# Block kernel, delta-rule layers: z and output units reordered behind the rule, and three taps per chunk moved out of it

## The reference, cut to what matters

```
h = rms_norm(x, norm_w);  proj = h @ w_in
qkv, z_a, a_lg, b_lg, cf_val, cf_glu, z_b, gate_lg = split(proj)
# delta-rule branch: a 5 tap convolution, 4 heads of 128, both directions
o = gated_delta_chunked(forward) + flip(gated_delta_chunked(backward))
o = o * rsqrt(mean(o * o, per head) + EPS) * dn_norm_w
y_a = (o * silu(z_a)) @ w_dn_out
# convolution branch: 31 taps along the sequence, per channel
u = cf_val * sigmoid(cf_glu)
u = depthwise_conv_centred(u, cf_conv_w) + cf_conv_b
u = silu(layer_norm(u, cf_ln_w, cf_ln_b))
y_b = (u * silu(z_b)) @ w_cf_out
y = gate_0 * y_a + gate_1 * y_b        # gates: sigmoid of gate_lg + bias
x = x + y @ w_out
```

## Time and profile before

| | us |
|---|---|
| median of 3 runs | 2148.33 |
| profiled execution | 2147.76 |
| its span (first to last instruction) | 2146.4 |
| PE busy in the span | 2067.1 (96%) |
| DVE / ACT / POOL busy | 1246.9 / 858.8 / 906.3 |
| layer 0: rule, then z and output units | about 1366 to 1512, 1512 to 1619 |
| layer 1: the same, 473.03 later | about 1839 to 1985, 1985 to 2092 |

### The profile page before, as it was taken

One profiled execution on the slowest core, in us unless ns is written; L12 is line 12 of the kernel. 1 busy time (PEld: TensorE's weight loads), 2 busy tenths in 40 slices (PEclk: granted clock), 3 DMA queues, 4 the chain that ended last, 5 costly groups with the idle time before them and its releaser, 6 DMA issues.

```text
span 2146.4 us, 26716 instructions
## 1 busy us (share of the span) xinstructions
PE 2067.1 (96%) x10774; PEld 1645.1 (77%) x10774; DVE 1246.9 (58%) x1943; ACT 858.8 (40%) x1373; POOL 906.3 (42%) x431
## 2 busy tenths in 40 slices
PE   9999999998999999999999899999999999999997
PEld 7888888775666688888888677787778787778775
DVE  6322223847677633222224988989753779898753
ACT  4222223324444543222234475444444375344632
POOL 4444444332213344444443564544434554444442
PEclk9999999999999999999999999999999999999999
DMA  4343333321101232333332222101223222100222
GB/s 160 109 136 98 98 98 101 106 69 40 31 25 56 69 98 89 98 98 98 98 96 91 78 79 69 59 31 31 69 80 97 89 81 77 50 25 26 79 89 78
DMA packets 46186, 169.09 MB, mean 79 GB/s; under 512 B 5232, under 2 KB 6000, under 8 KB 45808
## 3 DMA queue, kind: packets, MB, share of 16 engines
q1 hardware_dynamic: 45344, 165.60, 24.8%
q10 hardware_dynamic: 720, 1.79, 0.2%
HBM read 165.27 MB, written 2.10 MB: 78 GB/s over the span
## 4 chain that ended last, share of the span: by engine, by line
PE 74%; DVE 18%; ACT 5%; issue 1%; POOL 0%; DMA 0%; ACTq 0%; DVEq 0%
PE ps L385 21%; PE ps L386 21%; PE ps L387 21%; DVE cu L1843 4%; DVE blk_t L1945 2%; DVE outer L1943 1%; PE ps L639 1%; PE ps L655 1%; PE ps L624 1%; PE ps L441 1%; ACT whi L1009 1%; ACT dl L1441 1%; PE ps L959 1%; DVE dl L2052 1%; PE ps L970 1%
## 5 line engine op out<-in xcount | busy, mean ns | idle before, releaser
L2172 POOL TENSOR_TENSOR wlo<-raw,whi 128x1024 fp32r<-128x1024 f32 x300 | 750.9, 2510 | 863.9 <-ACT whi L1009 863.3
L385 PE MATMUL ps<-xh,whi 128*128 128x512 f32 x1584 | 640.3, 404 | 11.4 <-ACT gates L1185 6.2
L387 PE MATMUL ps<-xh,wlo 128*128 128x512 f32 x1584 | 619.7, 391 | 0.0
L386 PE MATMUL ps<-xl,whi 128*128 128x512 f32 x1584 | 619.3, 391 | 0.0
L1009 ACT CAST whi<-raw 128x1024 fp32r<-128x1024 f32 x300 | 312.6, 1044 | 167.9 <-DMA raw<-in_stream 167.8
L385 PEld LDWEIGHTS ps<-xh,whi 128*128 128x128 f32 x1584 | 298.6, 189 | 105.1 <-issue 32.3
L387 PEld LDWEIGHTS ps<-xh,wlo 128*128 128x128 f32 x1584 | 298.4, 188 | 63.6
L386 PEld LDWEIGHTS ps<-xl,whi 128*128 128x128 f32 x1584 | 298.9, 189 | 59.4 <-issue 2.9
L1843 DVE SCALAR_TENSOR_TENSOR cu<-up,lcols,cu 128x512 f32<-128x512 f32 x180 | 173.3, 1015 | 0.1
L2208 POOL TENSOR_TENSOR cu<-cu,prod 128x512 f32<-128x512 f32 x60 | 87.7, 1461 | 139.6 <-ACT prod L1252 138.5
L1548 DVE TENSOR_TENSOR ml<-mid,mh 128x512 fp32r<-128x512 f32 x42 | 57.5, 1372 | 151.5 <-ACT mh L1071 151.5
(11 more groups left out here) (360 smaller groups left out, 3000.8 us busy)
## 6 DMA issues: line engine op xcount, KB each, us to landing
raw<-in_stream SPq DMA_DIRECT2D x300, 512.0 KB, 3.6
w1k<-in_w SPq DMA_DIRECT2D x1, 2048.0 KB, 8.2
w1v<-in_w SPq DMA_DIRECT2D x1, 2048.0 KB, 8.1
outT<-h SPq DMA_DIRECT2D x4, 512.0 KB, 2.7
h<-in_xT SPq DMA_DIRECT2D x2, 512.0 KB, 7.9
h<-in_xT ACTq DMA_DIRECT2D x2, 512.0 KB, 7.5
mats<-in_mats ACTq DMA_DIRECT2D x1, 448.0 KB, 10.5
msk<-in_masks SPq DMA_DIRECT2D x1, 258.0 KB, 3.8
```

The lines of the kernel that those rows point to most:

```text
L385: pe.matmul(out, wh, hi, start=first, stop=False)
L386: pe.matmul(out, wh, lo, start=False, stop=False)
L387: return pe.matmul(out, wl, hi, start=False, stop=last)
L2172: pool.tensor_tensor(m.wlo[:, slot, :], m.raw[:, slot, :], m.whi[:, slot, :].bitcast(F32), ALU.subtract).then_inc(s.wlo)
```

## The change

1. `POINT_TAPS`: 11 taps a chunk instead of 14. The one at "decay" goes, "join1" 2 to 1, "keys" 4 to 3. `delta` returns the rest of the list.
2. The 8 output units of a layer become 4 of w_dn_out (41 to 44, called D0 to D3) and 4 of w_cf_out (48 to 51, C0 to C3). Each holds 2 column tiles by 4 tiles of the sum, again 24 matmuls. The order of units is now z0 to z4, D0 to D3, z5 to z7, C0 to C3, M0 to M7.
3. DVE behind the rule: 26 taps (2 of the last chunk, 24 more), `o_dn`, `times_z` with 2 taps before the last, `low_part` of `o`, and then 14 taps between the multiplications of the first gates with D0 to D3. In `merge` only the second product is left for each c.
4. PE's sums for the mean stand behind D3 instead of between z3 and z4, and only z5 is left between them and those for the variance.
5. ACT: `split_rows` of `o` directly after z3; casts of weights between c pairs in `merge`, one for each C unit. The mixer's merge of the first block keeps its form.

```diff
-L_QKV, L_GATE, L_Z, L_OUT, L_MERGE = 8, 20, 36, 44, 52
+L_QKV, L_GATE, L_Z, L_DN, L_CF, L_MERGE = 8, 20, 36, 41, 48, 52
...
-POINT_TAPS = {"decay": 1, "level1": 1, "join1": 2, "level2": 1, "join2": 2, "last": 1, "keys": 4, "out": 2}
+POINT_TAPS = {"level1": 1, "join1": 1, "level2": 1, "join2": 2, "last": 1, "keys": 3, "out": 2}
...
+
+
+def z_unit_at(l, n):
+    return U0_LAYER[l] + L_Z + n + (4 if n > 4 else 0)
...
# TensorE
+    def branch_unit(l, i, r):
+
+        u = U0_LAYER[l] + (L_DN, L_CF)[r] + i
+        pe.wait_ge(s.wlo, u + 1)
+        if i >= 2 and r == 0:
+            pe.wait_ge(s.sg, 16 + 8 * l + 2 * i - 2)
+        elif i >= 2:
+            pe.wait_ge(s.ysum, 8 + 8 * l + 2 * i - 2)
+        for rows in (range(3), (3,)):
+            for half in range(2):
+                for k in rows:
+                    if i == 0 and half == 0:
+                        pe.wait_ge(s.mix_lo, 8 + 8 * l + 4 * r + k + 1)
+                    ins = multiply(u, 4 * half + k, ps[:, 2 * (i % 2) + half, :], m.fh[:, 4 * r + k, :], m.fl[:, 4 * r + k, :],
+                                   k == 0, k == 3)
+        ins.then_inc(s.unit)
+
...
@@ -832,16 +860,18 @@
         z_unit(2)
         spread(3 * l + 3, range(4))
         z_unit(3)
+        z_unit(4)
+        pe.wait_ge(s.o_dn, 4 * l + 4)
+        for i in range(4):
+            branch_unit(l, i, 0)
         pe.wait_ge(s.conv, 3 * l + 3)
         pe.wait_ge(s.shared, 30 * l + 30)
         sum_rows(ps[:, 5, :], [m.cu[:, c, :] for c in range(4)]).then_inc(s.mean)
-        z_unit(4)
         z_unit(5)
         pe.wait_ge(s.cu_sq, 4 * l + 4)
         sum_rows(ps[:, 5, :], [m.rt[:, c, :] for c in range(4)]).then_inc(s.var)
         z_unit(6)
         z_unit(7)
-        pe.wait_ge(s.o_dn, 4 * l + 4)
 
     def gate_tiles(l, n, t0, t1):
 
...
# ScalarE
@@ -1374,14 +1404,16 @@
         z_unit(2)
         z_unit(3)
         weights_upto(u0 + L_Z + 4 + AHEAD + 1)
+        for k in range(4):
+            split_rows(k)
+        z_unit(4)
+        for i in range(4):
+            weights_upto(u0 + L_DN + i + AHEAD + 1)
         for c in range(4):
             act.wait_ge(s.cu_c, 4 * l + c + 1)
             act.activation(m.rt[:, c, :], m.cu[:, c, :], ACT.Square).then_inc(s.cu_sq)
-        z_unit(4)
         z_unit(5)
-        for k in range(4):
-            split_rows(k)
-        weights_upto(u0 + L_Z + 6 + AHEAD + 1)
+        weights_upto(z_unit_at(l, 6) + AHEAD + 1)
         act.wait_ge(s.var, l + 1)
         then(act.activation(ps[:, 5, :], ps[:, 5, :], ACT.Ln, bias=eps, scale=1.0 / (4 * P)))
         act.activation(ps[:, 5, :], ps[:, 5, :], ACT.Exp, scale=-0.5).then_inc(s.root_cu)
...
-            weights_upto(u0 + c + AHEAD + 1)
+            weights_upto(u0 + (c if mixer else c // 2) + AHEAD + 1)
...
# VectorE, merge
             p, bank = c % 2, 2 * (c % 2)
             if mixer:
                 dve.wait_ge(s.sg, 2 * c + 2)
+                dve.wait_ge(s.unit, u0 + c + 1)
             else:
-                dve.wait_ge(s.filled, 24 * g - 24 + (2 * c + 2))
-            dve.wait_ge(s.unit, u0 + c + 1)
+                dve.wait_ge(s.unit, u0 + c // 2 + 1)
             sg = [m.m1_sg[:, p, r, :] if mixer else m.sg[:, 2 * c + r, :] for r in range(2)]
-            for r in range(2):
-                t = step(dve.tensor_tensor(sg[r], sg[r], ps[:, bank + r, :], ALU.mult))
+            for r in range(2) if mixer else (1,):
+                at = bank + r if mixer else c % 4
+                t = step(dve.tensor_tensor(sg[r], sg[r], ps[:, at, :], ALU.mult))
...
-        delta(l, cf_tap)
+        taps = delta(l, cf_tap)
+
+        def conv(n):
+            for ch, k in taps[0:n]:
+                cf_tap(ch, k)
+            del taps[0:n]
+
+        conv(24)
...
@@ -2020,15 +2060,25 @@
             dve.wait_ge(s.z_used, 8 * l + n + 1)
             dve.tensor_tensor(m.fl[:, n, :], src, m.fh[:, n, :].bitcast(F32), ALU.subtract).then_inc(s.mix_lo)
 
+        for n in range(4):
+            if n == 3:
+                conv(2)
+            times_z(n)
+        for n in range(4):
+            low_part(n)
+        for c in range(KD):
+            if c % 2 == 0:
+                conv(4)
+                dve.wait_ge(s.filled, 24 * l + 2 * c + 4)
+                dve.wait_ge(s.unit, u0 + L_DN + c // 2 + 1)
+            dve.tensor_tensor(m.sg[:, 2 * c, :], m.sg[:, 2 * c, :], ps[:, c % 4, :], ALU.mult).then_inc(s.sg)
+        conv(len(taps))
+        dve.wait_ge(s.sg, 16 + 8 * l + 8)
         dve.wait_ge(s.conv, 3 * l + 3)
         dve.wait_ge(s.mean, l + 1)
         for c in range(4):
             dve.scalar_tensor_tensor(out=m.cu[:, c, :], in0=ps[:, 5, :], scalar=-1.0 / (4 * P), in1=m.cu[:, c, :],
                                      op0=ALU.mult, op1=ALU.add).then_inc(s.cu_c)
-        for n in range(4):
-            times_z(n)
-        for n in range(4):
-            low_part(n)
         dve.wait_ge(s.root_cu, l + 1)
         for c in range(4):
             dve.tensor_tensor(m.cu[:, c, :], m.cu[:, c, :], ps[:, 5, :], ALU.mult).then_inc(s.cu_n)
```

More of the change, by code:

```diff
@@ L709, in attention, with mixer_branches @@
         gates(turns + 1)
[L711 to L715, removed]
+    def branch_unit(l, i, r):
[13 more added lines that the diff above has]
+        ins.then_inc(s.unit)
+    def mixer_branches():
+        u0 = U0_MIX + 32
         for c in range(KD):
@@ L718, in merge @@
             if c >= 2:
-                pe.wait_ge(s.ysum, 8 * g + c - 1)
+                pe.wait_ge(s.ysum, c - 1)
             pe.wait_ge(s.wlo, u0 + c + 1)
@@ L723, in merge @@
                     if c == 0:
-                        pe.wait_ge(s.mix_lo, 8 * g + 4 * r + k + 1)
-                    ins = multiply(u0 + c, 4 * r + k, ps[:, bank + r, :], fh[:, 4 * r + k, :], fl[:, 4 * r + k, :],
+                        pe.wait_ge(s.mix_lo, 4 * r + k + 1)
+                    ins = multiply(u0 + c, 4 * r + k, ps[:, bank + r, :], m.xh[:, 4 * r + k, :], m.xl[:, 4 * r + k, :],
                                    k == 0, k == 3)
             ins.then_inc(s.unit)
-        u0 += 8
+    def merge(g):
+        mixer = g == 0
+        if mixer:
+            mixer_branches()
+        else:
+            for i in range(4):
+                branch_unit(g - 1, i, 1)
+        u0 = U0_MIX + 40 if mixer else U0_LAYER[g - 1] + L_MERGE
         y = m.m1_y if mixer else m.m2_y
@@ L823, in z_unit @@
         def z_unit(n):
-            u = u0 + L_Z + n
+            u = z_unit_at(l, n)
             pe.wait_ge(s.filled, 24 * l + GATE_UNITS + n - (1 if n < 2 else 2))
@@ L1215, in merge @@
         mixer = g == 0
-        u0 = U0_MIX + 32 if mixer else U0_LAYER[g - 1] + L_OUT
+        u0 = U0_MIX + 32 if mixer else U0_LAYER[g - 1] + L_CF
         if mixer:
@@ L1393, in layer @@
         z_unit(7)
-        weights_upto(u0 + L_OUT + AHEAD + 1)
+        weights_upto(u0 + L_CF + AHEAD + 1)
         for k in range(4, 8):
@@ L2083, in conv @@
         def conv(point):
-            n = POINT_TAPS[point]
+            n = POINT_TAPS.get(point, 0)
             for ch, k in taps[0:n]:
@@ L2135, in delta @@
             conv("out")
-        for ch, k in taps:
-            cf_tap(ch, k)
+        return taps
     dve.memset(m.ups[:, 0, 0:P], 0.0)
@@ L2343, in layout @@
         gates = pairs(proj(g[:, 0]), proj(g[:, 1]))
-        out = np.concatenate([proj(x["w_dn_out_2"][l]), proj(x["w_cf_out_2"][l])], 2)
-        units += [pairs(proj(glu), proj(val)), proj(qkv)[QKV_ORDER], gates, proj(za), proj(zb),
-                  out, proj(x["w_out_2"][l])]
+        dn, cf = (proj(x[n][l]).reshape(4, 2, P, 4 * P).transpose(0, 2, 1, 3).reshape(4, P, UNIT)
+                  for n in ("w_dn_out_2", "w_cf_out_2"))
+        units += [pairs(proj(glu), proj(val)), proj(qkv)[QKV_ORDER], gates, proj(za), proj(zb)[0:1], dn, proj(zb)[1:4],
+                  cf, proj(x["w_out_2"][l])]
     stream = np.concatenate(units)
```

## The result

| | kernel before | changed kernel |
|---|---|---|
| median, us | 2148.63 (4 runs, 2143.5 to 2149.21) | 2171.91 (4 runs, 2171.27 to 2172.55) |
| profiled execution, span, us | 2146.4 | 2169.9 |
| mean granted clock | 0.991 | 0.984 |

The ratio is 1.0115, with a 95% interval of 1.0099 to 1.0131: slower by about 1.2%, beyond the 0.3% that a measurement of this kernel can tell. The forecast was 2169 (2153 to 2181), slower with 0.81.

The account below looks back on a forecast made before the run. PE, busy for 96% of the span, was taken to bound the kernel, so only its idle time could change. Terms summed to +9.55 us a layer, +19.1 for two, plus 2 for the clock: about 2169 us, range 2153 to 2181.

Parts of the forecast that it names:

- the rule: Chunks 1 to 3 of the rule: PE's wait for the masked copy goes, a gain of 4.3 us a layer.
- z4 and D0's start: Behind the rule: POOL's low parts hold up two `times_z`, so D0 starts late; loss 3.5 us a layer.
- mean's sums: Behind D3: the sums wait for taps held up by POOL's low parts; net loss 0.8 us a layer.
- to C0's end: C0 begins with the tile that waits, 4.8 us, and loses 6.1 instead of 3.34: +2.75 us a layer.
- C1 to M0's last tile: In `merge`, POOL's low parts hold up the sums of c2, c4 and c6; loss 6.8 us a layer, bounds 1.1 and 6.8.
- clock, elsewhere: Half-clock stretches after three longer waits a layer: +2 us for both layers, bounds 0 and +10.
- rival B: Each new PE wait is followed by a half-clock stretch, +10 us instead of +2: 2177, up to 2184; chance 0.10.
- A: Half the collisions: only the merge's, 2157 us, or only D0's, 2155 us; chance 0.20.
- C: No collision of DVE and POOL: -0.95 us a layer, 2146 us, no change; chance 0.10.
- D: Taps gone from the rule remove all 7.2 us of PE's waits there, no collisions behind it: 2140 us; chance 0.07.

Follow-up runs that it names:

- e2: The changed kernel with the old table of taps and 12 taps instead of 24 ahead of `o_dn`; 2172.92 us.
- e5: The kernel before with the tap at "decay" gone and seven instead of four at "keys", 16 a chunk; 2134.81 us.
- e4: The changed kernel with POOL's subtraction for the weights of D0, D1, C3, M0 and M1 replaced by a memset to zero; 2144.23 us.
- e7: The changed kernel with the merge's steps in pairs, no tap at "decay", 16 taps a chunk, and 4 taps ahead of `o_dn`; 2142.53 us.
- e3: The changed kernel with DVE's merge steps in pairs: both products, both sums, both low parts of two c; 2154.99 us.
- e1: The kernel before with only the new table of taps, 11 a chunk instead of 14, order of units as before; 2158.02 us.
- e6: e5 with the variance's sums one z unit earlier, between z4 and z5, and ACT's steps reordered to suit; 2127.60 us.
- e8: e7 with the mean's sums before D3 and the variance's before z5, each one unit earlier; 2135.11 us.

## Why the prediction was right, term by term

| term, us a layer | predicted | measured in layer 0 |
|---|---|---|
| the rule | -4.3 | -5.0 (R) |
| z4 and D0's start | +3.5 | +3.8 (listed waits of 0.21 and 3.13) |
| mean's sums | +0.8 | -0.7 (no wait) |
| to C0's end | +2.75 | +3.6, part of it clock |
| C1 to M0's last tile | +6.8 | +7.4, part of it clock |
| clock, elsewhere | +1 | +2.7 in D0 to D3, +0.8 in M |
| sum | +10.55 | +12.6 of 12.6 |

The measured ones go from start to start of matmuls, since a wait costs PE a little more than the idle time listed for it. That time counts from the end of the last matmul (0.39 long), while at full speed the next one would start 0.23 behind its start, and the first ones behind a wait come more slowly. D0's start: z4's last matmul starts at 1538.28 and D0's first at 1541.80, where 1538.51 was due, so 3.3 for the listed 3.13. z4, with its wait of 0.21, takes 5.94 (from 1532.57 to 1538.51) instead of 5.44, 0.5 more. Mean's sums: 1537.66 in the kernel before, where 1537.00 was due. C0's end: due at 1589.59 behind z7, C0 is followed by C1 at 1601.94, so 12.35 against 8.78 before. C1 to M0: M0's last tile starts at 1629.63 and the next unit at 1631.08, so 29.1 from 1601.94, against four units of 5.44. D0 to D3 take 1566.30 - 1541.80 = 24.5, against 21.8. The 0.8 is what M takes more behind M0. Layer 1 lost 10.3 in all; its R gained 6.5 since a half-clock stretch at 1838 to 1848 (0.83) is no longer in it.

The total is closer than its terms. The clock term was 2.5 a layer too low and three others 0.3 to 0.8 too low, while the mean's sums were 1.5 and the rule 0.7 too high, and layer 1 got back 1.6 of clock that no term foresaw. That the sum came within 3 us of the measurement is in part luck; that four of the five places and their waits were the right ones is not.

**The rule.** Right in cause (e2 has the wait back, e5 loses it again), 0.7 short in size. The waits of 4.3 are gone whole, as I took it. The other 0.7 is again what a wait costs beyond its listed idle time: in chunks 1 to 3 the way from the products ahead of the masked copy (L887 x32, at 1487.17 in chunk 3) to the first gate tile behind it (1492.43) takes 5.26 in the kernel before and 3.60 in the changed one (1484.45 to 1488.05). That is 1.66 for a listed 1.44, three times a layer: 5.0.

**D0 and the port.** Right, and e4 shows the cause by removing it. I had the POOL operations in the right order: unit 40 (7.93 long), then 41 and 42, and two `times_z` held up.

**The mean's sums.** Wrong in sign, small. Four taps at 1543.38 took 6.97, 4.3 too long, for two POOL operations. I had counted three or four of them on the taps; the other two fell mostly where DVE waited for PE or read PSUM (four taps at 1556.89 took 2.87, two at 1562.33 took 1.70). D0 to D3 took 2.7 longer at the half clock, which gave DVE time. It is not the whole reason: in e2 and e7, with D0 to D3 at full clock (21.8), the sums wait nothing in layer 0 and 0.7 in layer 1, where I took 1.3.

**C0.** The wait came as worked out (4.69 for 4.8). I then let its first four tiles take 1.2 each, DVE's pace. In the new order only three tiles follow each other with a low part each (`rows` in `branch_unit`), and they took 1.42, 1.28 and 1.28 because at the half clock a tile takes 1.28. DVE's pace was hidden beneath it.

**The merge.** The surest reading of the traces. The sums of c2, c4 and c6 start 7.3 apart (1608.31, 1615.60, 1622.93) as in the working, and M0's last two tiles, which wait for the low parts of c6 and c7, started 25.0 and 27.7 behind C0's end for 25.1 and 27.8. The waits in M0 are 3.43 and 1.05 instead of 4.3 and 2.0. The 4.3 does not follow from the working: its seventh tile is due at 11.7 + 5.44 + 6 x 0.68 = 21.2 and waits to 25.1, which is 3.9. The second wait is shorter since the seventh tile, at the half clock, took 1.45 instead of 0.68. The part that the working left even without a collision, 1.1 a layer (its own 5.7 - 4.8 gives 0.9), is what e4 shows: M 1.1 longer than before. What I had not seen is that the loss is not bound to the order: e3 takes it away with the same units.

**The clock.** The mis-sized term: +2 for both layers, where D0 to D3 alone lost 2.7 and M 0.8 in layer 0. The three new waits, of 3.1 to 4.7, each had a half-clock stretch with them, so rival B's mechanism is true. Its price of +10 was too high here; part of each stretch fell in the wait itself, where it costs nothing. In layer 1 the stretches are there again, some shorter: the clock of 2025 to 2030 was 0.66, of 2076 to 2084 0.57, of 2110 to 2118 0.57.

Rivals A and C fall with the rows of the port: the five collisions forecast (two `times_z`, three sums) occurred, in both layers. D falls with the wait of 2.9 at L945 (L915 before), which stays in every kernel run here.

Of the page of the Trainium skill weighed there (SBUF — State Buffer, Who interferes with whom) the runs tell more: e1, e5 and the changed kernel again show taps that began after POOL's request pass it, 24, 4 and 8 of them, against issue order as the one thing that decides.

## What to carry to other kernels

A change that moves steps behind a stage is paid for in the queue of the engine that was late there, so work out its new timeline with the operations of the other port user laid beside it: here pairing the steps of the merge, so that no sum begins during a 2.4 us subtraction, gave back about 17 of 23 us. Before taking work out of a critical stage, ask which one instruction stands in front of the wait; e5 kept more taps in the rule than the kernel before and gained all of the 5 us. And put a reduction whose result needs a long chain (19 us) as early as its input allows, with independent units behind it (e6), instead of reordering the units around its end.

## What the runs showed of the hardware

**How long POOL stays shut out.** One subtraction of POOL (128x1024, 2.4 alone) requested in a run of taps (SCALAR_TENSOR_TENSOR with two SBUF sources) ended 2.3 behind the start of `o_dn`, which reads PSUM, as if it had run only then. With 4, 8, 12 and 24 taps begun after it (e5, changed, before, e1) it took 5.28, 7.93, 10.54 and 18.48: 2.64 and 0.66 for each tap. The rows of e5, the changed kernel and e1:

```profile
1520.38 5.28 POOL L2172 TENSOR_TENSOR wlo<-raw,whi 128x1024 fp32r<-128x1024 f32 x1 [6.81 <-ACT whi L1009]
```
```profile
1524.87 7.93 POOL L2221 TENSOR_TENSOR wlo<-raw,whi 128x1024 fp32r<-128x1024 f32 x1 [6.81 <-ACT whi L1039]
```
```profile
1526.45 18.48 POOL L2172 TENSOR_TENSOR wlo<-raw,whi 128x1024 fp32r<-128x1024 f32 x1 [6.83 <-ACT whi L1009]
```

(The 7.93 is the first of the three in the row of 13.11 above.) In other places the taps gave way. The changed kernel has both in one run of 26 taps: the low part at 1515.54 took 2.52, the next, at 1524.87, 7.93; and in e8 six taps took 8.34. What decides between the two is open: no run here tries it by itself.

**Long waits and the clock.** Every wait of PE of 3 us and more in the two layers of these kernels had a stretch with it in which the granted clock stood at 0.50: D0's 3.13, C0's 4.69, M0's 3.43, e1's 8.44. Shorter waits came both ways, so no length divides them here. Beside e8's wait of 2.8 in layer 0 the clock stayed at 1.00 (1540 to 1575); a little behind the end of its wait of 2.5 in layer 1 (2024.2) it was 0.50. The same wait of 1.9 before the output unit's fifth tile has such a stretch in layer 1 of the kernel before and none in layer 0. e6 has no wait of PE in 1500 to 1680 and stays at 1.00.

```profile
2025.60:2028.80 3.20, 3.20 (x5) 1.33 (x4) 0.00 (x0) 0.00 (x0) 0.00 (x0) 0.50 0.00 0
```

A wait of 3 to 5 us came with up to 2.7 more here, and removing it gave more than its length (e4: 26.2 in T and M, where the waits removed add up to about 15).
